# Feed-forward gate and up products with the weights stationary from step 1 on, in a two-block fp32 kernel on one Trainium2 core

## What is computed

```python
def rms_norm(x, gain):
    xf = x.astype(jnp.float32)
    y = xf * lax.rsqrt(jnp.mean(xf * xf, axis=-1, keepdims=True) + NORM_EPS)
    return (y * gain.astype(jnp.float32)).astype(x.dtype)

def swiglu(x, wg, wu, wd):
    return (jax.nn.silu(x @ wg) * (x @ wu)) @ wd
...
x = x + 0.5 * rms_norm(swiglu(rms_norm(x, g_ffn1_pre[l]), ffn1_wg[l], ffn1_wu[l], ffn1_wd[l]),
                       g_ffn1_post[l])
```

## Time and profile before

| what | us |
|---|---|
| median of 3 runs | 2799.02 (2797.6 to 2799.38) |
| the profiled execution | 2797.09 |
| its span in the profile | 2795.3 |
| TensorE (PE) busy | 2757.2 |
| VectorE (DVE) busy | 1685.1 |
| ScalarE (ACT) busy | 1450.8 |
| TensorE's granted clock | 0.999 of full speed |

### The profile page before, as it was taken

The page is one execution under the profiler, slowest core; times in us unless marked ns, Lnnn a source line. Parts: engine busy times, 40 slices in busy tenths (PEclk is TensorE's granted clock), DMA queues, the critical chain, the costliest instruction groups (busy, mean ns, idle before and its releaser), DMA issues.

```text
span 2795.3 us, 35866 instructions
## 1 busy us (share of the span) xinstructions
PE 2757.2 (99%) x13412; PEld 2300.7 (82%) x13412; DVE 1685.1 (60%) x2005; ACT 1450.8 (52%) x2021; POOL 188.2 (7%) x89
## 2 busy tenths in 40 slices
PE   8999999999999999999999999999999999999999
PEld 6888888888888888888888888888888888888887
DVE  4457757546546766555545779564555567875545
ACT  4446555445446555545445557554454475665444
POOL 0000000001001000100000221010010012210100
PEclk9999999999999999999999999999999999999999
DMA  6555445555565345555555544445555654454553
GB/s 213 192 172 182 135 156 168 195 187 185 191 200 179 127 149 174 182 190 173 196 189 199 164 136 151 151 152 197 193 179 182 206 181 137 146 170 136 181 181 120
DMA packets 315005, 481.86 MB, mean 172 GB/s; under 512 B 15376, under 2 KB 196112, under 8 KB 314640
## 3 DMA queue, kind: packets, MB, share of 16 engines
q1 hardware_dynamic: 314896, 480.37, 51.8%
HBM read 479.26 MB, written 1.05 MB: 172 GB/s over the span
## 4 chain that ended last, share of the span: by engine, by line
PE 90%; DVE 5%; ACT 3%; POOL 1%; issue 0%; DMA 0%; SPq 0%; ACTq 0%; DVEq 0%
PE bank L325 80%; PE bank L1360 2%; DVE w_low L311 2%; PE bank L700 1%; PE bank L426 1%; POOL w_low L317 1%; ACT w_high L306 1%; PE bank L680 1%; PE bank L341 1%; PE bank L1393 0%; DMA raw<-in_ffn_wu 0%; PE bank L1355 0%; PE bank L907 0%; PE bank L693 0%; PE bank L694 0%
## 5 line engine op out<-in xcount | busy, mean ns | idle before, releaser
L311 DVE TENSOR_TENSOR w_low<-raw,w_high 128x2048 fp32r<-128x2048 f32 x438 | 1018.2, 2327 | 559.1 <-ACT w_high L306 558.9
L306 ACT ACTIVATE w_high<-raw 128x2048 fp32r<-128x2048 f32 x451 | 861.9, 1914 | 545.8 <-PE bank L325 528.7
L325 PE MATMUL bank<-w_high,xT_high 128*128 128x512 f32 x2624 | 1040.0, 396 | 10.8 <-DVE w_low L311 9.2
L325 PE MATMUL bank<-w_high,xT_low 128*128 128x512 f32 x2624 | 1023.5, 390 | 0.0
L325 PE MATMUL bank<-w_low,xT_high 128*128 128x512 f32 x2624 | 1022.9, 390 | 0.0
L325 PEld LDWEIGHTS bank<-w_high,xT_high 128*128 128x128 f32 x2624 | 493.4, 188 | 117.8 <-DVE w_low L311 9.6
L325 PEld LDWEIGHTS bank<-w_high,xT_low 128*128 128x128 f32 x2624 | 493.1, 188 | 105.0
L325 PEld LDWEIGHTS bank<-w_low,xT_high 128*128 128x128 f32 x2624 | 493.7, 188 | 98.7
L468 ACT ACTIVATE silu<-bank,rstd 128x256 f32<-128x256 f32 x176 | 73.8, 471 | 288.5 <-PE bank L325 288.5
L325 PE MATMUL bank<-w_high,hT_high 128*128 128x512 f32 x640 | 206.4, 404 | 0.0
L325 PE MATMUL bank<-w_high,hT_low 128*128 128x512 f32 x640 | 199.2, 392 | 0.0
(11 more groups left out here) (268 smaller groups left out, 2482.4 us busy)
## 6 DMA issues: line engine op xcount, KB each, us to landing
raw<-in_w_in SPq DMA_DIRECT2D x288, 512.0 KB, 4.6
raw<-in_ffn_w_in SPq DMA_DIRECT2D x176, 512.0 KB, 4.6
raw<-in_ffn_wg SPq DMA_DIRECT2D x88, 512.0 KB, 3.9
raw<-in_ffn_wu SPq DMA_DIRECT2D x88, 512.0 KB, 4.8
raw<-in_ffn_wd SPq DMA_DIRECT2D x88, 512.0 KB, 4.1
raw<-in_ffn_w_out SPq DMA_DIRECT2D x88, 512.0 KB, 4.1
raw<-in_w_out SPq DMA_DIRECT2D x32, 512.0 KB, 4.6
raw<-in_w_branch_a SPq DMA_DIRECT2D x16, 512.0 KB, 4.5
```

What stands on the lines that cost most here:

```text
L306: nc.scalar.activation(wh[slot][:], raw[slot][:], ACT.Copy).then_inc(high_done[slot], 1)
L311: nc.vector.tensor_tensor(wl[slot][:], raw[slot][:], wh[slot][:].bitcast(F32), ALU.subtract).then_inc(low_done[slot], 1)
L325: mm = pe.matmul(o[:, 0:n], x[:, rows], w[slot][:, col + j * n:col + (j + 1) * n], start=start and first, stop=stop and last)
```

## The change

Step 0 stays as it was. From step 1 on the weights are stationary: `BLOCKS` are the four groups of 128 weight columns (gate 0, up 0, gate 1, up 1), one bank each (0 to 3). For each block and each half of the K tiles, four products of 512 columns have the high weights stationary and the high and low activations moving side by side; then four of 256 columns have the low weights stationary and the high activations moving. For that `xh` and `xl` are now interleaved in one tile `xT_parts`. Each bank then holds two sums of 256 tokens side by side, hidden features on the partitions. VectorE adds the two halves (`added`, a reduction over a view with a stride of 256 elements). Since tokens now lie along the free dimension, 1/rms must be a row: ScalarE writes a diagonal of `rstd`, a product with ones makes the row, ScalarE copies it to `frow`. The hidden tile comes out already turned, so `turn` is left for step 0 alone, now in banks 4 and 5. VectorE's order becomes: first half of hidden, low(sa), second half of hidden, low(sb), low part of hidden, low(sd).

```diff
-                    for k in range(4):
-                        kt = 4 * half + k
-                        mm = product(pe, [[acc[0][tt]] for tt in range(TT)], xh[:, kt, :], xl[:, kt, :],
-                                     s, k * 512, 512, kt == 0, kt == KT - 1)
+                    for n, (bank, col) in enumerate(BLOCKS):
+                        if half == 0 and first and n == 2:
+                            pe.wait_ge(hid_done, at(lay, 2, f + 1))
+                        if half == 0 and not first:
+                            pe.wait_ge(block_out, at(lay, 8 * (FSTEPS - 1), 4 * (FSTEPS - 1) * f + n - 7) + i * 4)
+                        for k in range(4):
+                            kt, w = 4 * half + k, slice(k * 512 + col, k * 512 + col + P)
+                            pe.matmul(bank[:], wh[s][:, w], xhl[:, kt, :, :], start=kt == 0, stop=False, skip_group_check=True)
+                        for k in range(4):
+                            kt, w = 4 * half + k, slice(k * 512 + col, k * 512 + col + P)
+                            mm = pe.matmul(bank[:, 0:SEQ], wl[s][:, w], xhl[:, kt, 0, :], start=False, stop=kt == KT - 1, skip_group_check=True)
+                        if half == 1 and n < 3:
+                            mm.then_inc(block_done, 1)
+                        if half == 0 and first and n == 0:
+                            pe.wait_ge(fdiag_done, at(lay, 2, f + 1))
+                            pe.wait_ge(sums_set, 1)
+                            pe.matmul(ps[6][:, 0:SEQ], ones, fdiag[:], start=True, stop=True).then_inc(frow_done, 1)
+                        if half == 0 and first and n == 1:
+                            turn()
...
             with pe.Fori(2, FSTEPS - 1) as i:
                 up(i)
-                down(i - 1, 0, sd, False, False)
-                turn(i)
-                down(i - 1, 1, sd, False, False).then_inc(slot_used[sd], 1)
+                for k in range(2):
+                    mm = down(i - 1, k, sd, False, False)
+                mm.then_inc(slot_used[sd], 1)
...
             for k in range(2):
                 down(last - 1, k, sd, False, False, tiles=(0,))
-            turn(last)
             down(last - 1, 0, sd, False, False, tiles=(1,))
...
+            for tt in range(TT):
+                a = nc.scalar.activation(fdiag[:, tt, :], ident, ACT.Copy, scale=rstd[:, tt:tt + 1])
+            a.then_inc(fdiag_done, 1)
...
-                silu(i)
+                silu(i, 0)
+                silu(i, 1)
                 split_high(act, blk, sb, lay, b[sb] + 1 + i)
-                turn_high(i)
+                high(i)
                 split_high(act, blk, sd, lay, b[sd] + 1 + i)
...
+            def added(dst, bank):
+                return nc.vector.tensor_reduce(dst, bank[:].rearrange("p (a n) -> p n a", a=2), AX.X, ALU.add).then_inc(block_out, 1)
+
+            def hidden(i, h):
...
+                dve.wait_ge(block_done, three + i * 3)
+                added(gT[:, h, :], BLOCKS[2 * h][0])
+                dve.wait_ge(block_out, four + i * 4)
+                nc.vector.tensor_tensor(gT[:, h, :], gT[:, h, :], frow[:], ALU.mult).then_inc(gate_in, 1)
...
+                added(uT[:, h, :], BLOCKS[2 * h + 1][0])
+                dve.wait_ge(silT_done, two + i * 2)
+                nc.vector.tensor_tensor(sT[:, h, :], sT[:, h, :], frow[:], ALU.mult).then_inc(silr_done, 1)
...
+                nc.vector.tensor_tensor(hidT[:, h, :], sT[:, h, :], uT[:, h, :], ALU.mult).then_inc(hidT_done, 1)
```

More of the change, by code:

```diff
@@ L457, in ffn_act @@
             b = [ffn_use(blk, f, s) for s in range(SLOTS)]
-            def silu(i):
-                first = isinstance(i, int) and i == 0
-                sums = acc[first]
-                if first:
-                    s = LEAD[1]
-                    act.wait_ge(slot_used[s], use(blk, s, lay, b[s] + 1))
-                else:
-                    act.wait_ge(slot_used[sb], use(blk, sb, lay, b[sb] + 1) + i)
-                for tt in range(TT):
-                    a = nc.scalar.activation(sil[:, tt, :], sums[tt][:, 0:FC], ACT.Silu, scale=rstd[:, tt:tt + 1])
-                a.then_inc(silu_done, 1)
@@ L493, in ffn_act @@
+            high(FSTEPS - 1, hTh_last)
             split_high(act, blk, sb, lay, b[sb] + FSTEPS)
-            turn_high(FSTEPS - 1, hTh_last)
         def ffn_dve(dve, blk, lay, f):
@@ L501, in low @@
                 split_low(dve, blk, slot, lay, b[slot] + k)
-            def hidden(i):
-                sums = acc[isinstance(i, int) and i == 0]
-                dve.wait_ge(silu_done, at(lay, 22, FSTEPS * f + 1) + i)
-                for tt in range(TT):
-                    h = nc.vector.scalar_tensor_tensor(hid[:, tt, :], sums[tt][:, FC:2 * FC], rstd[:, tt:tt + 1],
-                                                       sil[:, tt, :], ALU.mult, ALU.mult)
-                h.then_inc(hid_done, 1)
@@ L519, in ffn_dve @@
+            for tt in range(TT):
+                h = nc.vector.scalar_tensor_tensor(hid[:, tt, :], acc[1][tt][:, FC:2 * FC], rstd[:, tt:tt + 1],
+                                                   sil[:, tt, :], ALU.mult, ALU.mult)
+            h.then_inc(hid_done, 1)
             low(sb, 1)
+            for k in range(2):
+                dve.wait_ge(hTh_done, at(lay, 44, 2 * FSTEPS * f + k + 1))
+                nc.vector.tensor_tensor(hTl[:, k, :], ps[4 + k][:, 0:SEQ], hTh[:, k, :].bitcast(F32), ALU.subtract).then_inc(hTl_done, 1)
@@ L531, in ffn_dve @@
+            low_part(FSTEPS - 1, hTh_last, hTl_last)
             low(sb, FSTEPS)
```

87 lines of the change are left out of this document (59 added, 28 removed).

## The result

The changed kernel takes 2792.7 us (median of 16 runs, 2791.11 to 2794.8) beside 2798.43 us of the kernel before (16 runs, 2796.63 to 2800.08): a ratio of 0.998, 95% interval 0.9972 to 0.9988. The gain is 5.7 us, half of the 10.4 forecast, and the time lies inside the range. The profiled execution took 2791.78 us, its span is 2790.0 us (before 2795.3), its granted clock 0.999 as before.

A forecast was written before the change was run, and what follows sets the result against it. TensorE, busy 99% of the span, was taken as the bound, so only what it issues counts in the loop. Terms -35.2 + 17.0 + 3.4 + 3.2 + 1.2 = -10.4 us gave 2788.6 us, range 2780 to 2805.

The forecast's parts named there:

- part 1: Feed-forward steps 1 to 10: transposes gone from TensorE's path, 0.44 us each group, 35.2 us less.
- part 2: Feed-forward steps: two 256-column products cost 0.0133 us more than one of 512, 17.0 us more in all.
- part 3: Start of each feed-forward call: the product making the 1/rms row costs 0.43 us, 3.4 us more in all.
- part 4: Loop: VectorE's new chain, 13.3 us in a step of 16.6, makes TensorE wait for nothing.
- part 5: End of a call: TensorE waits for the last hidden tile, 3.2 us more; block 1's post delayed, 1.2 us more.
- Rival C: Start of each call: diagonal, silu, hidden or first split late, TensorE waits; +8 us, 2796.6 us; chance 16%.
- rival A: VectorE's strided PSUM reduction takes 1.24 us, so TensorE waits longer at call ends: 16.4 us more, 2805.0 us; chance 15%.
- Rival B: Loop products: only columns count, the narrow pairs cost nothing extra; -27.4 us, 2771.6 us; chance 7%.

The follow-up runs named there:

- the turned version: Kernel with wide then narrow products in both halves and ScalarE's earlier split, its second half turned to narrow first: 2781.12 us, ratio 0.9941.
- step 10 doubled: The changed kernel with the four bank reductions of step 10 alone done twice: 2823.03 us, ratio 1.0084.
- doubled loop: The changed kernel with every bank reduction of the loop (steps 1 to 9) done twice: 2798.47 us, ratio 1.0004.

## Why the prediction was right, and where it was not

**The sign and the place.** The gain is told from no change (0.9972 to 0.9988 excludes 1), and it lies in the loops' TensorE stream, as argued from the busy share and the chain. The forecast missed by 4 us. How near it came was in part luck, as the table shows. In the table the measured terms come from differences of mean steps and calls in the traces.

| term | predicted us | measured us | from |
|---|---|---|---|
| part 1, transposes | -35.2 | -38.1 | 80 x (16.849 - 16.373) |
| part 2, widths | +17.0 | +28.2 | 80 x (16.725 - 16.373) |
| part 3, row product | +3.4 | +3.5 | the eight calls without it |
| part 4, loop | 0 | 0 | no waits, steps equal when doubled |
| part 5, wait for the last hidden tile | +3.2 | 0 | no such row |
| part 5, post delayed | +1.2 | +1.0 | 4 x 0.26 |
| sum | -10.4 | -5.4 | measured -5.6 in the calls |

**Part 2 is the step that failed.** I took 0.1200 for a narrow product from a stretch of narrow ones and 0.2267 for a wide one from a stretch of wide ones. Each is right in its own company: in the turned version the sum of just these (16 x 0.2267 = 3.63, 16 x 0.1200 = 1.92) is on the chain. The error was to carry them over to a stream in which they alternate by fours, where the wide ones cost 0.2322 and the narrow ones 0.1184. The difference is 11 us, more than the miss of the whole sum. The narrow ones do not make up for it. I had no bound between "free" and the transposes' 0.154. A row that would have warned stands in the kernel before: its transposes are narrow products (128 columns), and `up`, which opens 12 down products behind them, begins with spacings of 235, 228, 232 and 230 ns (means over the loop turns) before it settles at 227. In the kernel without transposes these four are 227 too. I read the earlier trace rows from the settled part. The Trainium skill, "TensorE: Matmul & The Clock Gate", section "Back-to-back issue gap", has a formula, meant for a product taken by itself, that would have made the term 3.2 us; measured 28.2, so the trace disagrees more than I said.

**Part 1** was 3 us too small: the 0.44 on the chain is what the four transposes take, but their neighbours had been spaced wider too.

**Part 3** held, with its slack. ScalarE's diagonal begins at 28.89 in the changed kernel's first call and its silu at 29.49; then hidden and the transposes (timeline; idle time before in brackets):

```profile
30.34 0.88 DVE L562 SCALAR_TENSOR_TENSOR hidden<-bank,rstd,silu 128x256 f32<-128x256 f32 x2 [2.05 <-ACT silu L501]
...
32.01 0.60 PE L449 MATMUL bank<-konst,hidden 128*128 128x128 f32 x4
```

Hidden ends at 31.22, the transposes begin at 32.01: 0.8 us of slack, 0.6 predicted. Rival C did not occur.

**Part 4** and **rival A** hang on the reduction with its stride in PSUM. Its group in the changed kernel (busy us, mean ns, idle before):

```profile
L532 DVE TENSOR_REDUCE gateT<-bank 128x256 f32<-128x512 f32 x160 | 110.0, 688 | 155.1 <-PE bank L426 155.1
```

0.688 us, beside 0.683 for the contiguous read of as many elements and my 0.68; two summands 1 KB apart cost nothing. Rival A is excluded, and with it the statement of the Trainium skill, "Advanced Engine Details and Errata", section "PSUM Cachelines", as carried over to a read by VectorE: the trace does not agree with it there. VectorE's busy time per step is 12.41 us, where I had 13.3 with gaps.

**Part 5.** The end of the first call in the changed kernel, VectorE and TensorE (start us, us, engine, what):

```profile
194.95 0.42 DVE L556 TENSOR_TENSOR hT_low_last<-hiddenT,hT_high_last 128x256 fp32r<-128x256 f32 x1
...
195.50 0.65 PE L335 MATMUL bank<-w_high,hT_high_last 128*128 128x512 f32 x2
```

TensorE comes to the last hidden tile at 195.50, 15.36 us after the first product of step 10 (I had 15.2), and its low part ended at 195.37, 15.23 (I had 15.5, since each of VectorE's instructions starts some 0.08 us before the one ahead of it ends). So where I had forecast a wait of 0.4 us there is a slack of 0.13: the mechanism is there, as step 10 doubled showed, but the term of 3.2 us is nought. The second half of part 5 did occur:

```profile
197.33 2.29 DVE L321 TENSOR_TENSOR w_low<-raw,w_high 128x2048 fp32r<-128x2048 f32 x1 [1.39 <-ACT w_high L316]
...
198.49 0.60 ACT L635 ACTIVATE squares<-bank 128x512 f32<-128x512 f32 x1 [1.19 <-PE bank L335]
...
199.54 0.69 DVE L655 TENSOR_TENSOR post<-bank,kblk 128x512 f32<-128x512 f32 x1
```

`post` could have started at 198.49 + 0.79 = 199.28 and starts at 199.54, behind low(sb): 0.26 us in each of the four calls of block 1, and just the difference between the gains of the two blocks' calls (0.57 and 0.83). With low(sb) out of its way (the variant with ScalarE's earlier split) these calls got 0.21 to 0.27 us back.

**Rival B** (only columns count, part 2 at nothing) is out: part 2 measured 28 us. The errors of parts 1 and 5 (-2.9 and -3.2) hid more than half of that of part 2 (+11.2). That was luck: the forecast was nearer than its largest term deserved.

## What to carry to other kernels

Take the spacing of products from a stretch with the same neighbours; where none is in the trace, give the mix a range of its own. If products of two widths must share a stream, gather each width in long runs and change over as seldom as the banks allow: here that alone gave back 8.5 of 11 us (7.5 by sorting, 1.0 by turning the second half, from the calls). Products strictly in turn did as well or better in 24 turns of 64 (16.59 us against 16.607) and worse in the other 40, so measure every turn and not one. A step whose chain on another engine is within 0.2 us of being wanted should be priced on both sides, and dear on the late side, since a stalled TensorE came back at a lower clock in seven calls of eight here.

## What the runs showed that I had not expected

- Wide products are slower for some five places behind narrow ones (233 to 236, 228, 232, 230 ns against 226.7), even across 24 down products, and a narrow one right behind wide ones is quicker (113 to 118 against 120 ns).
- Strictly alternating products of two widths ran at two levels, 16.59 and 16.79 to 16.80 us a step, with the same instructions.
- After a wait of 1.8 us TensorE's granted clock fell to 0.5 for about 3.4 us in seven calls and not in the eighth; after the wait of 2.46 us for `o_diff` it fell in the profile of the changed kernel and not in that of the kernel before; during one of 4.3 us and behind it, it was at 0.5 for 6.8 us. The changed kernel's waits of up to 0.8 us at `x_res` show no such drop. So the length of a wait alone does not tell whether the clock falls.
- One instruction of VectorE (x_res) took 5.05 us instead of 0.75 where GpSimd's low part began at the same moment, and with the clock lost behind it that cost 6.5 us. A doubled loop that left every step unchanged thus came out 0.2% slower; only the comparison call by call told the two apart. The changed kernel has the same two instructions only 0.13 us apart there, in the harmless order.
